# Attention inside a two-layer trunk: scores as split fp32r products, the next pair's projections spread over eight steps

## The reference

```python
def chunk_causal_attention(q_nope, q_rope, k_nope, k_rope, v):
    ...
        s = (jnp.einsum('bqhd,bkhd->bhqk', qn, k_nope)
             + jnp.einsum('bqhd,bkd->bhqk', qr, k_rope)).astype(jnp.float32) * scale
        s = jnp.where(key_chunk[None, :] <= q_chunk[:, None], s, -jnp.inf)   # chunks of 64
        p = jax.nn.softmax(s, axis=-1).astype(v.dtype)
        return jnp.einsum('bhqk,bkhv->bqhv', p, v)           # blocks of 128 queries
def mla_mixer(h, positions, w_in, q_norm, w_uq, kv_norm, w_ukv, w_out):
    c_q, c_kv, k_rope = split_cols(h @ w_in, ODD_SPLITS)     # 384, 256, 64
    q = (rmsnorm(c_q, q_norm) @ w_uq).reshape(B, T, MLA_HEADS, MLA_NOPE + MLA_ROPE)
    kv = (rmsnorm(c_kv, kv_norm) @ w_ukv).reshape(B, T, MLA_HEADS, MLA_NOPE + MLA_V)
    ...                                                      # q_rope, k_rope are rotated
    return chunk_causal_attention(q_nope, q_rope, k_nope, k_rope, v) @ w_out
```

## Time and profile before

| | us |
|---|---|
| median of 3 runs (lowest, highest) | 1284.05 (1282.94, 1287.27) |
| the profiled execution, its time | 1281.99 |
| its span | 1280.3 |
| PE busy, share of the span | 1230.2, 96% |
| DVE busy | 657.8, 51% |
| ACT busy | 519.7, 41% |
| first score matmul starts | 768.66 |
| last group of transposes starts | 869.24 |

### The profile page before, as it was taken

One profiled execution on the slowest core, in us unless ns is written; L12 is line 12 of the kernel. 1 busy time (PEld: TensorE's weight loads), 2 busy tenths in 40 slices (PEclk: granted clock), 3 DMA queues, 4 the chain that ended last, 5 costly groups with the idle time before them and its releaser, 6 DMA issues.

```text
span 1280.3 us, 16203 instructions
## 1 busy us (share of the span) xinstructions
PE 1230.2 (96%) x5995; PEld 997.3 (78%) x5995; DVE 657.8 (51%) x1034; ACT 519.7 (41%) x1009; POOL 113.4 (9%) x126
## 2 busy tenths in 40 slices
PE   6899999969999999999999999999999999999997
PEld 5677788857988888888887875557788888888886
DVE  4466877754663443443447236562644343443444
ACT  4544565434632332323336753332642232332332
POOL 2231313300280000000000001000000000000000
PEclk9999999989999999999999999999999999999999
DMA  3322122114332222223223222100322322223321
GB/s 119 101 81 67 51 58 59 50 49 148 108 115 94 89 100 97 98 98 98 99 83 91 68 64 82 43 1 17 130 100 99 97 98 92 92 99 98 99 83 66
DMA packets 87443, 108.22 MB, mean 85 GB/s; under 512 B 9138, under 2 KB 48147, under 8 KB 87380
## 3 DMA queue, kind: packets, MB, share of 16 engines
q1 hardware_dynamic: 85684, 101.85, 24.8%
q0 software_dynamic: 1696, 5.51, 1.2%
HBM read 104.20 MB, written 2.10 MB: 83 GB/s over the span
## 4 chain that ended last, share of the span: by engine, by line
PE 84%; DVE 7%; ACT 6%; issue 2%; DMA 1%; DVEq 0%; POOL 0%; SPq 0%; ACTq 0%
PE bank L1385 24%; PE bank L1387 24%; PE bank L1386 24%; PE po L1785 1%; PE pp L1768 1%; PE pp L1767 1%; PE pp L1525 1%; PE pp L1428 1%; ACT w_hi L467 1%; ACT w_hi L469 1%; DVE w_lo L477 1%; PE po L1536 1%; PE pp L1386 0%; PE pp L1387 0%; PE pp L1385 0%
## 5 line engine op out<-in xcount | busy, mean ns | idle before, releaser
L1385 PE MATMUL bank<-h_lo,w_hi 128*128 128x512 f32 (+4 forms) x572 | 217.8, 381 | 8.7 <-DVE h_lo L1018 4.4
L1387 PE MATMUL bank<-h_hi,w_hi 128*128 128x512 f32 (+4 forms) x572 | 215.4, 377 | 0.0
L1386 PE MATMUL bank<-h_hi,w_lo 128*128 128x512 f32 (+4 forms) x572 | 215.2, 376 | 0.0
L1385 PE MATMUL bank<-wx,a_hi 128*128 128x512 f32 x320 | 126.0, 394 | 5.1 <-DVE wx L477 5.1
L1385 PEld LDWEIGHTS bank<-h_lo,w_hi 128*128 128x128 f32 (+1 forms) x572 | 106.8, 187 | 30.8 <-DVE h_lo L1018 4.9
L1387 PE MATMUL bank<-wx,a_hi 128*128 128x512 f32 x320 | 124.7, 390 | 0.0
L1386 PE MATMUL bank<-wx,a_lo 128*128 128x512 f32 x320 | 124.6, 389 | 0.0
L1241 DVE TENSOR_TENSOR tmp<-sq,bank 128x512 f32<-128x512 f32 x64 | 44.0, 688 | 155.9 <-ACT sq L879 155.9
L1387 PEld LDWEIGHTS bank<-h_hi,w_hi 128*128 128x128 f32 (+1 forms) x572 | 106.6, 186 | 19.7
L1386 PEld LDWEIGHTS bank<-h_hi,w_lo 128*128 128x128 f32 (+1 forms) x572 | 106.8, 187 | 18.5
L879 ACT ACTIVATE sq<-bank 128x512 f32<-128x512 f32 x64 | 38.3, 598 | 204.3 <-PE bank L1387 204.3
(11 more groups left out here) (286 smaller groups left out, 2037.7 us busy)
## 6 DMA issues: line engine op xcount, KB each, us to landing
stage<-in_mlp_w SPq DMA_DIRECT2D x128, 512.0 KB, 3.6
stage<-in_ev_w_in SPq DMA_DIRECT2D x28, 512.0 KB, 3.6
stage<-in_ev_w_out SPq DMA_DIRECT2D x8, 512.0 KB, 3.6
stage<-in_od_w_out SPq DMA_DIRECT2D x8, 512.0 KB, 3.6
stage<-in_od_w_in SPq DMA_DIRECT2D x10, 256.0 KB, 3.0
x_tok<-in_x SPq DMA_DIRECT2D x4, 512.0 KB, 5.0
gbc<-in_norm_gains POOLq DMA_DIRECT2D x4, 512.0 KB, 4.4
xr<-in_x POOLq DMA_DIRECT2D x1, 2048.0 KB, 9.1
```

Of the source, the lines that this page charges most:

```text
L1385: nc.tensor.matmul(dst, wh, xl_, start=first, stop=False)
L1386: nc.tensor.matmul(dst, wl, xh, start=False, stop=False)
L1387: return nc.tensor.matmul(dst, wh, xh, start=False, stop=last)
```

## The change

The arithmetic of the scores is split like the rest. The content queries and keys are kept as high and low parts: `key(h)` and `query(h)` name free tiles of `a_hi`/`a_lo` and `h_hi`/`h_lo` and one new pair, `k_last`. The content score becomes `mm3`, three fp32r matmuls. The rotary score becomes two fp32r matmuls over 128 rows: `q_rope` holds the high part in one half of the rows and the low part in the other, and `kr` (in both halves) comes as a high and a low version. The mask is fp32r. The copies into `y` that ACT made alone are now two: high on ACT, low on DVE, and PE's next tile in that bank waits for DVE's. The turned probabilities go to `y`, which is free now, in two alternating halves by head; DVE still copies them.

The next pair's projection is taken apart: `qr` comes first (its unit is loaded first), PE projects it at step 0 of the eight after that step's scores, the two `qn` tiles at steps 3 and 5. ACT and DVE have their parts at steps 1, 2, 4, 5, 6 and 7. On PE the transposes now come before the values. ACT reads a head's output at j % 4 == 3 instead of 2, DVE at j % 4 == 0.

```diff
...
-            p_t = sb("p_t", [P, NT, T], F32, s3)
-            kr = sb("kr", [P, T], F32, s3)
+            q_rope = sb("q_rope", [P, 2, 2, T], F32R, s3)
+            kr = sb("kr", [P, 2, T], F32R, s3)
+            k_last = sb("k_last", [P, 2, T], F32R, s3)
             cosd = sb("cosd", [P, T], F32, s3)
             sind = sb("sind", [P, T], F32, s3)
             ang = sb("ang", [P, T], F32, s3)
             prob = sb("prob", [P, 3, T], F32, s3)
-            qr = sb("qr", [P, 2, T], F32, s3)
-            mask_q = sb("mask_q", [P, P], F32, s3)
-            mask_k = sb("mask_k", [P, P], F32, s3)
+            q_sum_f32 = sb("q_sum_f32", [P, T], F32, s3)
+            mask_q = sb("mask_q", [P, P], F32R, s3)
+            mask_k = sb("mask_k", [P, P], F32R, s3)
             stat = sb("stat", [P, 4, 4 * MLA_HEADS], F32, s3)
 
...
+        def turned_probs(h):
+            return y[:, NT * (h % 2):NT * (h % 2) + NT, :]
+
+        def key(h):
+            if h < MLA_HEADS - 2:
+                return a_hi[:, KV_RANK_T + h, :], a_lo[:, KV_RANK_T + h, :]
+            if h == MLA_HEADS - 2:
+                return h_hi[:, KD - 1, :], h_lo[:, KD - 1, :]
+            return k_last[:, 0, :], k_last[:, 1, :]
+
+        def query(h):
+            c = Q_RANK_T + h % 4
+            return h_hi[:, c, :], h_lo[:, c, :]
...
                 if a >= 1:
-                    pool.wait_ge(qr_ready, a)
+                    pool.wait_ge(qr_sum, a)
...
+            def query_high(h):
+                n = tile_no[("qn", h // 2, h % 2)]
+                wait_tile(act, n)
+                nc.scalar.activation(query(h)[0], bank[n % 2][:, :], ACT.Copy).then_inc(qn_high, 1)
+
+            def key_high(h):
+                n = tile_no[("mk", h // 4, h % 4)]
+                wait_tile(act, n)
+                nc.scalar.activation(key(h)[0], bank[n % 2][:, :], ACT.Copy).then_inc(kt_high, 1)
+            def rope_high(a):
+                act.wait_ge(qr_sum, a + 1)
                 for hh in range(2):
+                    r = ROPE_ROWS[hh]
+                    nc.scalar.copy(q_rope[r, a % 2, hh, :], q_sum_f32[r, :]).then_inc(qr_high, 1)
...
+            pump(unit_no[("qr", 0)])
+            query_high(0)
+            query_high(1)
+            pump(unit_no[("qn", 0)])
+            for h in range(MLA_HEADS):
+                key_high(h)
+                if h == 4:
+                    rope_high(0)
+                if h == 5:
+                    pump(unit_no[("mk", 0)])
+            pump(unit_no[("mk", 1)])
...
+                a, step = j // 8 + 1, j % 8
+                if a < MLA_HEADS // 2:
+                    if step == 1:
+                        pump(unit_no[("qr", a)])
+                    elif step == 4:
+                        query_high(2 * a)
+                    elif step == 5:
+                        rope_high(a)
+                    elif step == 6:
+                        query_high(2 * a + 1)
+                        pump(unit_no[("qn", a)])
+                if j >= 7 and j % 4 == 3:
                     att_out(j // 4 - 1)
             att_out(MLA_HEADS - 1)
...
-            ch.link(nc.vector.tensor_tensor(kr[:, :], flat[0], cosd[:, :], ALU.mult))
+            ch.link(nc.vector.tensor_tensor(q_sum_f32[:, :], flat[0], cosd[:, :], ALU.mult))
             ch.link(nc.vector.tensor_tensor(ang[:, :], flat[1], sind[:, :], ALU.mult))
-            nc.vector.tensor_tensor(kr[:, :], kr[:, :], ang[:, :], ALU.add).then_inc(rope_ready, 1)
-            def kv_pump(what):
-                for g in range(2):
-                    wait_tile(dve, tile_no[(what, g, 3)])
-                    pump(unit_no[(what, g)])
+            ch.link(nc.vector.tensor_tensor(q_sum_f32[:, :], q_sum_f32[:, :], ang[:, :], ALU.add))
...
+            def key_low(h):
+                hi, lo = key(h)
+                dve.wait_ge(kt_high, h + 1)
+                nc.vector.tensor_tensor(lo, bank[tile_no[("mk", h // 4, h % 4)] % 2][:, :], hi.bitcast(F32),
+                                        ALU.subtract).then_inc(kt_ready, 1)
+
+            def query_low(h):
+                hi, lo = query(h)
+                dve.wait_ge(qn_high, h + 1)
+                nc.vector.tensor_tensor(lo, bank[tile_no[("qn", h // 2, h % 2)] % 2][:, :], hi.bitcast(F32),
+                                        ALU.subtract).then_inc(qn_ready, 1)
...
+            def rope_low(a):
+                for hh in range(2):
+                    dve.wait_ge(qr_high, 2 * a + hh + 1)
+                    r, other = ROPE_ROWS[hh], ROPE_ROWS[1 - hh]
+                    nc.vector.tensor_tensor(q_rope[other, a % 2, hh, :], q_sum_f32[r, :],
+                                            q_rope[r, a % 2, hh, :].bitcast(F32), ALU.subtract).then_inc(qr_ready, 1)
...
+            rotate(0)
+            pump(unit_no[("qr", 0)])
+            query_low(0)
+            query_low(1)
+            pump(unit_no[("qn", 0)])
+            for h in range(MLA_HEADS):
+                key_low(h)
+                if h == 3:
+                    rotated(0)
+                if h == 5:
+                    pump(unit_no[("mk", 0)])
+                    rope_low(0)
+            pump(unit_no[("mk", 1)])
+
...
                     i = j - 2
-                    qb = i % 4
+                    h, qb = divmod(i, 4)
                     dve.wait_ge(pt_done, i + 1)
-                    nc.vector.tensor_copy(p_t[:, 0:qb + 1, qb * P:(qb + 1) * P],
-                                          t_bank[i % 2][:, 0:qb + 1, :]).then_inc(pt_ready, 1)
-                if j >= 6 and j % 4 == 2:
-                    att_out(j // 4 - 1)
+                    if qb == 0 and h >= 2:
+                        dve.wait_ge(pv_done, h - 1)
+                    nc.vector.tensor_copy(turned_probs(h)[:, 0:qb + 1, qb * P:(qb + 1) * P],
+                                   t_bank[i % 2][:, 0:qb + 1, :]).then_inc(pt_ready, 1)
+                a, step = j // 8 + 1, j % 8
+                if a < MLA_HEADS // 2:
+                    if step == 1:
+                        rotate(a)
+                    elif step == 2:
+                        pump(unit_no[("qr", a)])
+                    elif step == 4:
+                        rotated(a)
+                    elif step == 5:
+                        query_low(2 * a)
+                    elif step == 6:
+                        rope_low(a)
+                    elif step == 7:
+                        query_low(2 * a + 1)
+                        pump(unit_no[("qn", a)])
+                if j >= 8 and j % 4 == 0:
+                    att_out(j // 4 - 2)
             att_out(MLA_HEADS - 1)
             split_low(dve, OO + SPLIT)
             linear_out("oo", 2, OO, MLP[1][1])
...
-                    pe.wait_ge(qr_ready, a + 1)
-                    wait_read(pe, tile_no[("qn", a, 1)])
+                if qb == 0:
+                    pe.wait_ge(qr_ready, 2 * a + hh + 1)
+                    pe.wait_ge(qn_ready, h + 1)
                 if j == 0:
                     pe.wait_ge(kt_ready, MLA_HEADS)
-                nc.tensor.matmul(dst[:, 0:width], qr[r, a % 2, s], kr[r, 0:width], start=True, stop=False)
-                nc.tensor.matmul(dst[:, 0:width], qn[:, a % 2, hh, s], y[:, h, 0:width], start=False, stop=False)
+                q_hi, q_lo = query(h)
+                k_hi, k_lo = key(h)
+                for part in range(2):
+                    nc.tensor.matmul(dst[:, 0:width], q_rope[:, a % 2, hh, s], kr[:, part, 0:width], start=part == 0,
+                                     stop=False)
+                mm3(dst[:, 0:width], q_hi[:, s], q_lo[:, s], k_hi[:, 0:width], k_lo[:, 0:width], False, False)
                 nc.tensor.matmul(dst[:, width - P:width], mask_q[:, :], mask_k[:, :], start=False,
                                  stop=True).then_inc(s_done, 1)
 
@@ -1782,21 +1864,26 @@
                 if h >= 1:
...
             for j in range(4 * MLA_HEADS + 2):
-                if j % 8 == 0 and j // 8 + 1 < MLA_HEADS // 2:
-                    project_q(j // 8 + 1)
                 if j < 4 * MLA_HEADS:
                     scores(j)
+                a, step = j // 8 + 1, j % 8
+                if a < MLA_HEADS // 2:
+                    if step == 0:
+                        project_qr(a)
+                    elif step in (3, 5):
+                        project_qn(2 * a + step // 4)
+                if 2 <= j:
+                    transposes(j - 2)
                 if j >= 6 and j % 4 == 2:
                     values(j // 4 - 1)
-                if 2 <= j:
-                    transposes(j - 2)
 
             def oo_first():
```

101 lines of the change are left out of this document (40 added, 61 removed).

## The result

The changed kernel took 1268.4 us (median of 6 runs, 1264.76 to 1273.47) against 1282.94 (6 runs, 1277.82 to 1287.27): ratio 0.989, 95% interval 0.987 to 0.991. The forecast was 1268. Its profiled execution was the longest of the six: 1273.47 us, span 1271.7.

A forecast was written before the change was run, and what follows sets the result against it. PE was taken to bound the attention, afterwards the loop through the values. Gains of 12 us in the heads and 2.5 before them, 14.5 off 1281.99 or the median 1284.05, gave 1267.5 or 1269.5; forecast 1268, range 1259 to 1277.

The forecast's parts named there:

- Price of the split scores: PE's score matmuls: 0.23 us at 512 columns, 0.11 at 128; a head's scores fall from 6.4 to 3.6 us.
- Rival D: PE's scores: switching between fp32r and float32 costs 0.3 us, 64 switches 19 us, leaving about 1284 to 1288; chance 3%.
- The loop through the values: DVE maximum to copy, PE values, 512-key scores, next maximum: 9.25 us per head without projections, against 10.52 before.
- Rival A: Attention: PE's work alone decides, 81 us with waits, a gain of 20 there, total about 1260; chance 10%.
- First head of a pair: Head with both content tiles at steps 3 and 5: the loop plus 1.5 and 0.6 us, about 11.3.
- Second head of a pair: Head with weight split and rotary tile: 9.25 us of loop plus 1.8 of DVE's work, about 11.0.
- The block's stall goes: Spread projections: the second pair's 28.50 us loses its 2.2 of waiting; two heads with projections then take 22.3.
- Before the first scores: Key stage and first projections: first scores 2.5 us earlier than 768.66, bounds 5 us earlier to none.
- The 3 us for small hand-overs: Allowance added to the heads' 85.5 us sum, giving 88.5 from first scores to last transposes.
- The sixth loop: Sixth of seven stretches between 512-wide row maxima: put at 11.0 us, like the other second heads.
- Rival C: Attention: PE's waits lower the clock; eight losses cancel the gain, from nine or ten on 1284 to 1295; chance 5%.
- Rival B: Heads: each of seven loops 1 us longer, nothing gained before the first scores, total 1277 to 1279; chance 22%.

The follow-up runs named there:

- experiment 4: Changed kernel with each head's values and their output one step later, values behind the 512-key scores on PE: ratio 0.9843 to the kernel before.
- 5: Changed kernel with PE's scores issued one step ahead of the transposes: ratio 0.9824 to the kernel before.
- experiment 6: Changed kernel with each head's values cut to their diagonal, 512 of 1280 columns, part of the computation left out: ratio 0.9786 to the kernel before.
- 7: Changed kernel with the 512-wide copy of turned probabilities on ACT instead of DVE: ratio 0.9882 to the kernel before.
- 1: Kernel before with only the projections spread over steps 0, 3 and 5, first pair's rotary tile first, scores left float32: ratio 0.9993 to the kernel before.
- 2: Kernel before with projections spread and the first queries' turning put ahead of the weight splits in DVE's queue: ratio 0.9946 to the kernel before.
- kernel 12: Changed kernel with scores one step ahead, the sixth key's weight split behind the eighth, and the 512-wide probability copy on ACT: 1258.18 us, ratio 0.980.
- 8: Changed kernel with outputs read a step earlier again, as before the change: ratio 0.9899 to the kernel before.
- 9: Changed kernel with values one step later and one weight split moved from behind the sixth key to behind the eighth: ratio 0.9823 to the kernel before.
- 11: Changed kernel with values one step later, scores one step ahead and the weight split behind the eighth key: ratio 0.9881 to the kernel before.
- 10: Changed kernel with scores one step ahead and the weight split moved from behind the sixth key to behind the eighth: 1256.96 us, ratio 0.980.
- kernel 3: Changed kernel with each next pair's projections put back in one block, scores still split: ratio 0.9947 to the kernel before.

## Why the prediction held, and where not

- **Price of the split scores**: right. 0.23 us at 512 columns and 0.11 at 128, in groups of five as elsewhere. Rival D was about the switch to float32 and back: from the mask at 845.29 over two float32 transposes to the next fp32r product at 845.50 pass 0.21 us, less than its 0.3 for one switch, so it is out.
- **The loop through the values**: right for the last head, which has no projections: 9.20 against 9.25. Experiments 4, 5, 6 and 7 each cut or stretched that loop, and the last head followed by -1.14, -1.72, -1.26 and +0.22 us. Rival A needed PE's busy time to decide: PE was busy 7.61 of 9.20.
- **First head of a pair**: 11.06 and 11.08 for a forecast of 11.3; PE is full there, and cutting the values gave 1.5 us; moving them a step later gave 0.8 with the same work (experiment 4), so the order still counts beside PE's sum. The forecast sign that every maximum is released by PE failed for the maxima that end the second heads, as DVE bounds those.
- **Second head of a pair**: 10.99 and 10.94 for 11.0, but the reason was only half right. I added the 1.8 us of DVE to the loop through the values; experiment 6 left the head at 10.86. DVE's own row of 10.6 to 10.7 us bounds it, and the loop lay at nearly the same length beside it (7 lengthened it by 0.2). The step to mend: sum the engine's own row of a head (10.7) first, then the loop, and take the longer.
- **The block's stall goes**: right. Spreading alone took the two heads from 28.5 to 26.3 us, the 2.2 of waiting that the forecast named; with the split scores they took 22.0. DVE's long waits for ACT's halves are gone. Experiments 1 and 2 show that this rests on the order in DVE's queue, not on spreading alone.
- **Before the first scores**: 1.7 us for 2.5. The two us for the split and the rotary low halves behind the sixth key are there (PE waits 2.33); moving the split behind the eighth gave 0.8 back.
- **The 3 us for small hand-overs** were mis-sized: from the first value matmul under the fall of the clock to the first content product behind it passed 5.29 us, in the next head 2.73 (rows at the end), so the fall cost at least 2.6 us, and without it the heads would have taken at most 84.6, where the bare sum was 85.5. The 85.5 held no fall; the one that came filled the allowance.
- **The sixth loop** was put at 11.0 like the other second heads, though PE has no projection there and DVE no turning (busy 8.30 us, in the others 10.6 to 10.7). It took 13.50 with the fall in it; with the scores ahead and no fall it took 8.48. What it takes in the changed kernel without a fall no run shows; 13.50 less the 2.6 leaves at most 10.9.
- **The number itself** owes something to luck. The sum was 14.5 us, and 14.5 lie between the medians; but it rests on a fall of the clock that filled an allowance made for something else, and 1268 was chosen between two values because the first median before (1284.05) was above the profiled execution.
- **Rival C**: no fall in every head. PE waits in each head and the granted clock was 1.00 in six loops of seven. So the sum by the Trainium skill's rule (TensorE: Matmul & The Clock Gate, "A second HAM failure mode: psum-queue depth-cycling"), a loss in every head, did not come about; the one fall that did cost at least 2.6 us. The sign named for C (a clock under 0.95 in the attention) did not show either, 0.96 from 770 to 858 us, if only just. **Rival B**: the maxima lay 11 us apart, not 12.

## What to carry to other kernels

When matmuls get cheap, look for the loop that goes through several engines in order, and sum it beside each engine's own row of work: the bound can differ from one step to the next. Such a loop is shortened by taking a piece out of it (issue the next scores a step ahead, or the values a step later), not by moving a piece to an idler engine (9.42 us instead of 9.20 in the last head). Moving it can pay where an engine's own row is the bound (10.86 to 10.28 in the second heads of kernel 12). Whatever is issued earlier must be checked against the youngest of its inputs, since it holds up all that is queued behind it.

## What the runs showed of the hardware

The granted clock fell in the sixth loop of the changed kernel, where PE has no projection left but DVE still has a weight split (windows of 2 us; length, PE, its loads, DVE, ACT, POOL; clock):

```profile
832.00:834.00 2.00, 1.28 (x13) 1.15 (x12) 1.87 (x6) 0.97 (x3) 0.00 (x0) 1.00 0.00 0
834.00:836.00 2.00, 0.78 (x8) 0.63 (x6) 1.96 (x5) 0.38 (x1) 0.00 (x0) 1.00 0.00 0
836.00:838.00 2.00, 1.32 (x9) 1.32 (x10) 1.97 (x6) 0.55 (x2) 0.00 (x0) 0.95 0.50 159
838.00:840.00 2.00, 1.72 (x5) 0.95 (x4) 1.89 (x8) 0.66 (x2) 0.00 (x0) 0.50 0.27 103
...
842.00:844.00 2.00, 2.00 (x7) 1.52 (x6) 0.00 (x0) 0.00 (x0) 0.00 (x0) 0.50 0.00 0
844.00:846.00 2.00, 2.00 (x13) 1.69 (x12) 0.44 (x1) 0.00 (x0) 0.00 (x0) 0.85 0.00 0
```

PE was busy 3.4 of the 6 us from 832 to 838; then the clock stood at its lower level (0.50, 1.2 GHz) for nearly 7 us, into which the eight value matmuls fell. The values and the first of the scores behind them, under the fall and in the next head:

```profile
839.32 4.63 PE L1867 MATMUL po<-y,v_tok 128*128 128x512 f32 x8
844.61 0.40 PE L1460 MATMUL pp<-h_lo,h_hi 128*128 128x512 f32 x1
...
851.08 2.42 PE L1867 MATMUL po<-y,v_tok 128*128 128x512 f32 x8 [0.27 <-DVE y L1432]
853.81 0.40 PE L1460 MATMUL pp<-k_last,h_hi 128*128 128x512 f32 x1
```

The place is hardly chance, though each kernel has one profile only. Those of kernels 4, 6, 7, 8, 9 and 11 have the same fall in the sixth loop, between 828 and 843 us, 3 to 7 us long. The three with the scores ahead and the values in place (5, 10, 12) have none in the heads' loops, nor have 1, 2 and 3. Part of what the scores ahead gain is thus the clock's. Another fall, between 765 and 775 us, follows PE's wait ahead of the first scores in 1, 8, 10 and 11; in 8 that wait was 2.32 us, and in the changed kernel, where it was 2.33, there was no fall. A short lull alone does not decide it: in kernel 3 PE was busy 3.0 us of 6 (818 to 824), and the clock stayed at 1.00. What does was not found.
